# Up projections with the weights stationary and the rounded rows and remainders of both token tiles streamed as one; a norm's sums and the middle dilated group moved

## What is computed

```python
def first_block(x, ...):
    proj = rmsnorm(x, ln1_g) @ w_in            # qa ka va | qb kb vb | gates
    oa = dilated_attention(qa, ka, va)         # 12 heads of 64, three groups of 4, one per dilation
    ob = banded_attention(qb, kb, vb)          # 8 query heads, 2 key heads
    x = x + (sigmoid(ga) * (oa @ w_branch_a) + sigmoid(gb) * (ob @ w_branch_b)) @ w_out
    return x + square(relu(rmsnorm(x, ln2_g) @ w_up)) @ w_down      # 1024 -> 4096 -> 1024

def swiglu(x, w_in, w_out):                    # 1024 -> 2 x 2816 -> 1024
    gate, up = split(x @ w_in)
    return (silu(gate) * up) @ w_out

def second_block(x, ...):                      # two layers
    x = layer_norm(ALPHA * x + 0.5 * swiglu(x, ffn1), g0, b0)
    x = layer_norm(ALPHA * x + hybrid_mixer(x), g1, b1)
    x = layer_norm(ALPHA * x + 0.5 * swiglu(x, ffn2), g2, b2)
```

## Time and profile before

| | |
|---|---|
| median of 3 runs | 1364.85 us (1364.48 to 1365.22) |
| profiled execution | 1365.28 us, its span 1363.5 us |
| PE (matmuls) | 1343.1 us busy, 99%, 6449 instructions |
| PEld (weight loads) | 1090.2 us busy, 80% |
| DVE | 834.2 us busy, 61%, 1170 instructions |
| ACT | 633.7 us busy, 46%, 900 instructions |
| POOL | 67.4 us busy, 5% |
| DMA | 238.03 MB at 175 GB/s, the queue q1 at 53.5% |

### The profile page before, as it was taken

The page is one execution under the profiler, slowest core; times in us unless marked ns, Lnnn a source line. Parts: engine busy times, 40 slices in busy tenths (PEclk is TensorE's granted clock), DMA queues, the critical chain, the costliest instruction groups (busy, mean ns, idle before and its releaser), DMA issues.

```text
span 1363.5 us, 15986 instructions
## 1 busy us (share of the span) xinstructions
PE 1343.1 (99%) x6449; PEld 1090.2 (80%) x6449; DVE 834.2 (61%) x1170; ACT 633.7 (46%) x900; POOL 67.4 (5%) x133
## 2 busy tenths in 40 slices
PE   8999999999999999999999999999999999999997
PEld 7878788888888888876788888888888867888886
DVE  6676667454455555687874444754446888754445
ACT  7765635444335333346543334443344466444441
POOL 3130000000000000000300000000000002000000
PEclk9999999999999999999999999999999999999999
DMA  9542255555556655552465655475555442755650
GB/s 299 192 143 93 94 202 199 182 189 184 188 180 209 191 189 192 184 148 82 148 225 188 192 190 188 142 243 187 193 190 169 157 122 85 254 187 187 190 177 31
DMA packets 149241, 238.03 MB, mean 175 GB/s; under 512 B 5496, under 2 KB 97680, under 8 KB 149168
## 3 DMA queue, kind: packets, MB, share of 16 engines
q1 hardware_dynamic: 148784, 236.48, 53.5%
q0 software_dynamic: 384, 0.54, 0.2%
HBM read 235.95 MB, written 1.05 MB: 174 GB/s over the span
## 4 chain that ended last, share of the span: by engine, by line
PE 89%; DVE 5%; DVEq 1%; POOL 1%; ACT 1%; issue 1%; DMA 1%; POOLq 0%; SPq 0%; ACTq 0%
PE ps L1405 26%; PE ps L1407 25%; PE ps L1406 25%; PE ps L1742 2%; PE ps L1454 2%; PE ps L1447 1%; PE ps L1448 1%; PE ps L1653 1%; DVE stats L1166 1%; PE ps L1549 1%; PE ps L1575 1%; PE ps L1435 1%; POOL lrs L489 1%; DVE xres L1162 1%; PE ps L1666 1%
## 5 line engine op out<-in xcount | busy, mean ns | idle before, releaser
L462 DVE TENSOR_TENSOR wlo<-raw,whi 128x2048 fp32r<-128x2048 f32 x179 | 405.4, 2292 | 114.1 <-ACT whi L454 114.1
L1405 PE MATMUL ps<-whi,xt_hi 128*128 128x512 f32 (+1 forms) x1056 | 422.5, 400 | 0.5 <-DVE wlo L435 0.5
L1407 PE MATMUL ps<-whi,xt_lo 128*128 128x512 f32 (+1 forms) x1056 | 409.5, 388 | 0.0
L1406 PE MATMUL ps<-wlo,xt_hi 128*128 128x512 f32 (+1 forms) x1056 | 408.4, 387 | 0.0
L454 ACT ACTIVATE whi<-raw 128x2048 fp32r<-128x2048 f32 x197 | 370.4, 1915 | 0.0
L1405 PEld LDWEIGHTS ps<-whi,xt_hi 128*128 128x128 f32 x1056 | 198.6, 188 | 50.3 <-issue 13.9
L1407 PEld LDWEIGHTS ps<-whi,xt_lo 128*128 128x128 f32 x1056 | 198.4, 188 | 41.4
L1406 PEld LDWEIGHTS ps<-wlo,xt_hi 128*128 128x128 f32 x1056 | 199.0, 188 | 35.3
L776 ACT ACTIVATE ht_hi<-ps 128x256 fp32r<-128x256 f32 (+1 forms) x104 | 38.2, 415 | 323.8 <-PE ps L1742 323.6
L1405 PE MATMUL ps<-whi,ht_hi 128*128 128x512 f32 x480 | 187.7, 391 | 0.0
L1407 PE MATMUL ps<-whi,ht_lo 128*128 128x512 f32 x480 | 187.0, 390 | 0.0
(11 more groups left out here) (209 smaller groups left out, 1203.2 us busy)
## 6 DMA issues: line engine op xcount, KB each, us to landing
raw<-in_ffn_w_in_dram SPq DMA_DIRECT2D x176, 512.0 KB
raw<-in_ffn_w_out_dram SPq DMA_DIRECT2D x44, 1024.0 KB
raw<-in_w_in_dram SPq DMA_DIRECT2D x36, 1024.0 KB
raw<-in_w_up_dram SPq DMA_DIRECT2D x16, 1024.0 KB
raw<-in_w_down_dram SPq DMA_DIRECT2D x16, 1024.0 KB
raw<-in_w_out_dram SPq DMA_DIRECT2D x8, 1024.0 KB
raw<-in_w_out_dram SPq DMA_DIRECT2D x8, 512.0 KB
ln_g<-in_ln_g_dram SPq DMA_DIRECT2D x7, 512.0 KB, 8.0
```

The source lines that it names most:

```text
L462: dve.tensor_tensor(wlo[j][:, :], raw[j][:, :], whi[j][:, :].bitcast(F32), ALU.subtract).then_inc(lo_done, 1)
L1405: pe.matmul(o, hi[:, k, tok], block_of(whi, u, b, width), start=start, stop=False)
L1406: pe.matmul(o, hi[:, k, tok], block_of(wlo, u, b, width), start=False, stop=False)
L1407: return pe.matmul(o, lo[:, k, tok], block_of(whi, u, b, width), start=False, stop=stop)
```

## The change

**Up projections.** All chunks but the first of the MLP and of each feed-forward now have the weights as the stationary operand. A unit of weights holds 8 blocks x 256 columns instead of 4 x 512 (`load_columns`). `up_unit` takes 128 hidden columns of it: for each of 8 blocks one matmul with the rounded weights stationary and `xt_both` moving, which is the 256 tokens' rounded rows and their remainders, 512 columns in two runs of 256; and one with the weights' remainder stationary and the 256 rounded rows moving, into the first half of the same bank. The bank then holds 128 hidden columns x 256 tokens twice, and DVE adds the halves (`up_sum`). The hidden values are already transposed, so `hid_tile_pe` runs for the first chunks alone. In a feed-forward DVE adds gate columns and up columns, ACT takes silu from SBUF (`gate_act`), DVE multiplies; in the MLP DVE does relu and square in one instruction. ACT copies the rounded part, DVE the remainder (`ht_rest`). Banks are freed by a new semaphore, `up_read`.

**Norms.** The add sums its row as it goes (accum_out), DVE makes the mean, ACT squares and sums (`norm_act`), POOL does two operations (`rsqrt`), and the centred rows have a buffer of their own, `cent`. Ahead of three of the six norms, those behind a feed-forward that splits the next part's first two units early (`after`), DVE's order changes as well.

**Dilated groups.** The two heads of each pair of the middle group change places (`read_proj1`, strips 0 and 2), so its product comes from the other 64 rows, and the groups' scores are stored in the order 0, 2, 1, 256 columns apart. The scores of step HALF are issued behind that step's first filling pieces. DVE splits the units of the attention's steps in halves, at twice as many steps.

Cut to its core, the diff:

```diff
-STEP_LO = {2: 16, 4: 17, 6: 18, 8: 19, 10: 20, 13: 21, 15: 22, 17: 23}
+STEP_LO = {1: (16, 0), 2: (16, 1), 3: (17, 0), 4: (17, 1), 6: (18, 0), 7: (18, 1), 8: (19, 0), 9: (19, 1), 10: (20, 0),
+           11: (20, 1), 12: (21, 0), 13: (21, 1), 14: (22, 0), 15: (22, 1), 16: (23, 0), 17: (23, 1)}
+DIL_ORDER = (0, 2, 1)
...
-        xt_hi = sb("xt_hi", [P, KD, TOK], F32R, at=at_xt)
-        xt_lo = sb("xt_lo", [P, KD, TOK], F32R, at=at_xt + 8 * KB)
+        xt_both = sb("xt_both", [P, 2, KD, TOK], F32R, at=at_xt)
+        xt_hi, xt_lo = xt_both[:, 0], xt_both[:, 1]
...
+        def load_columns(sp, u, w, col):
+            load(sp, u, rows_of(u, KD), w[:, :, col:col + BW // 2])
         def load_ffn_in(sp, u, w, s):
+            if s > 0:
+                for c in range(2):
+                    load_columns(sp, u + c, w, c * FF2 + s * FFN_H)
...
-                load_strip(sp, mlp_up(s), w_up_r, s * BW)
+                if s == 0:
+                    load_strip(sp, mlp_up(s), w_up_r, s * BW)
+                else:
+                    for j in range(2):
+                        load_columns(sp, mlp_up(s) + j, w_up_r, s * BW + j * BW // 2)
...
+            if u < U_BRANCH:
+                m = scaled_lo(dve, u, (2 * h, 2 * h + 1))
+            else:
+                m = dve.tensor_tensor(wlo[j][:, part], raw[j][:, part], whi[j][:, part].bitcast(F32), ALU.subtract)
...
-                pool.tensor_tensor(lrs[:, t:t + 1], lrs[:, t:t + 1], half[:, 0:1], ALU.pow).then_inc(lrs_ready, 1)
+                rsqrt(pool, lrs[:, t:t + 1], mv[:, t, 1:2], 1.0 / DM, EPS2 / ALPHA ** 2, lrs_ready)
...
+        def norm_act(act, q, t):
+            act.wait_ge(mean_ready, 2 * q + t + 1)
+            act.activation(squares[:, t, :], xres[:, t, :], ACT.Square, bias=nmean[:, t:t + 1],
+                           accum_out=mv[:, t, 1:2]).then_inc(var_ready, 1)
...
+            elif s == 0:
+                parts = [plain(0, BW // 2)] + [swapped(BW // 2, i) for i in range(4)]
+            elif s == 2:
+                parts = [swapped(0, i) for i in range(4)] + [plain(BW // 2, BW)]
...
+        def gate_act(act, g):
+            act.wait_ge(up_read, 2 * up_index(g) + 1)
+            act.activation(hid_b[:, 0, :], hid_a[:, 0, :], ACT.Silu).then_inc(hid_act, 2)
...
+        def up_sum(dve, j, k, n):
+            b = UP_BANKS[j] + k
+            return dve.tensor_reduce(hid_a[:, j, k * TOK:(k + n) * TOK].rearrange("p (k n) -> p k n", k=n),
+                                     ps[:, b:b + n, :].rearrange("p k (j n) -> p k n j", j=2), AX.X, ALU.add)
+        def ht_rest(dve, g, par, k, n, src, done, by):
+            dve.wait_ge(ht_hi_done, 2 * g + done)
+            dve.tensor_tensor(ht_lo[par][:, k:k + n, :], src, ht_hi[par][:, k:k + n, :].bitcast(F32),
+                              ALU.subtract).then_inc(ht_lo_done, by)
...
+            dve.wait_ge(used, u + ffn_up(e) + 1)
+            up_sum(dve, 0, 0, 2).then_inc(up_read, 1)
             split_lo(dve, u + ffn_down(e))
+            for k in range(2):
+                cols = slice(k * TOK, (k + 1) * TOK)
+                if k == 0:
+                    dve.wait_ge(up_tile, g // FFN_S + 1)
+                else:
+                    dve.wait_ge(used, u + ffn_up(e) + 2)
+                m = up_sum(dve, 1, k, 1)
+                if k == 1:
+                    m.then_inc(up_read, 1)
+                dve.drain()
+                dve.wait_ge(hid_act, hid_acts(g + e) + 2)
+                dve.tensor_tensor(hid_b[:, 1, cols], hid_a[:, 1, cols], hid_b[:, 0, cols], ALU.mult).then_inc(hid_ready, 1)
+                if k == 1:
+                    for v in after[:1]:
+                        split_lo_half(dve, v, 0)
+                ht_rest(dve, g + e, e % 2, k, 1, hidden2[:, k:k + 1, :], k + 1, 1)
             for v in after[:1]:
-                split_lo(dve, v)
-            hidden_dve(dve, g + e, e % 2, True, (0,))
+                split_lo_half(dve, v, 1)
             for v in after[1:]:
                 split_lo(dve, v)
-            ht_dve(dve, g + e, e % 2, True, (0,))
...
-                dve.scalar_tensor_tensor(xs, src, (0.5 if ffn else 1.0) / ALPHA, xs, ALU.mult, ALU.add)
-            def stat(t, h):
+                dve.scalar_tensor_tensor(xs, src, (0.5 if ffn else 1.0) / ALPHA, xs, ALU.mult, ALU.add,
+                                         accum_out=sums[:, t, h:h + 1])
+            def mean(t):
                 dve.drain()
-                dve.bn_stats(stats[:, t, h, :], xres[:, t, h * BW:(h + 1) * BW])
-            def variance(t):
+                dve.tensor_scalar(nmean[:, t:t + 1], sums[:, t, 0:1], sums[:, t, 1:2], -1.0 / DM,
+                                  ALU.add, ALU.mult).then_inc(mean_ready, 1)
...
+                dve.scalar_tensor_tensor(cent[:, t, :], xres[:, t, :], nmean[:, t:t + 1], ln_g[:, :], ALU.add, ALU.mult)
...
-                parts = [(h % 2, 2 * g + h // 2, 6 + 2 * g + h // 2) for g in range(DIL_G)]
+                parts = [(h % 2 ^ (g == 1), 2 * g + h // 2, 6 + 2 * g + h // 2) for g in range(DIL_G)]
...
-                c = i * (n if len(parts) == DIL_G else BW)
+                c = DIL_ORDER.index(i) * TOK if u < HALF else i * BW
...
-        def up_chunk(pe, u, par, between=None, at=None):
-            for k in range(KD):
-                if k % 4 == 0:
-                    pe.wait_ge(lo_done, u + k // 4 + 1)
-                for t in range(TT):
-                    m = tile_mm(pe, xt_hi, xt_lo, k, u + k // 4, k % 4, t, 2 * par + t, k == 0, k == KD - 1)
-                if k % 4 == 3:
-                    m.then_inc(used, 1)
-                if k == at:
-                    between()
+        def up_unit(pe, u, j, k):
+            o = ps[:, UP_BANKS[j] + k, :]
+            pe.wait_ge(lo_done, u + 1)
+            for b in range(KD):
+                cols = slice(b * BW // 2 + k * P, b * BW // 2 + (k + 1) * P)
+                pe.matmul(o.rearrange("p (j n) -> p j n", j=2), whi[SLOT_OF[u]][:, cols], xt_both[:, :, b, :],
+                          start=b == 0, stop=False)
+                m = pe.matmul(o[:, 0:TOK], wlo[SLOT_OF[u]][:, cols], xt_hi[:, b, :], start=False, stop=b == KD - 1)
+            return m
+        def up_chunk(pe, u, g, first=None, tile=False):
+            for j in range(2):
+                for k in range(2):
+                    if first is not None and j == 1:
+                        hid_tile_pe(pe, g - 1, k, first)
+                    elif k == 0 and up_index(g) > 0:
+                        pe.wait_ge(up_read, 2 * up_index(g) - 1 + j)
+                    m = up_unit(pe, u + j, j, k)
+                    if k == 1:
+                        m.then_inc(used, 1)
+                    elif tile and j == 1:
+                        m.then_inc(up_tile, 1)
...
-                if i < UNITS:
+                if i < UNITS and i != HALF:
...
+                if i == HALF:
+                    scores(pe, i)
```

## The result

The changed kernel takes **1357.62 us** (median of 4 runs, 1356.41 to 1358.07) against 1365.03 beside it: a ratio of 0.9942, with a 95% interval of 0.9927 to 0.9958. It is faster by 7.4 us where 16.7 were forecast, and 1357.62 lies just above the range. This span is short for its time: 3.1 us of the execution lie outside it, 1.8 in the one before and 2.0 to 2.1 in the other three of the changed kernel. So 8.8 is some 1.3 more than the 7.5 by which the times of the same two executions differ.

What follows compares the result with a forecast made beforehand. PE's own queue was taken to bound the kernel, with room on DVE and ACT. The terms 9.9 - 24.2 - 3.0 - 0.4 + 1.4 - 0.4 = -16.7 us gave 1348.3 us, range 1344 to 1357.

Steps and rivals of the forecast that it cites:

- The up projections' matmuls: In 47 changed chunks, 32 x 226.7 + 32 x 119.8 = 11.09 us replaces 10.88: +9.9 us.
- The transposes: Hidden-tile transposes leave PE's queue except after first chunks, 0.89 us each in the MLP, 0.45 in feed-forwards: -24.2 us.
- The cover on DVE and ACT: The new sums and splits on DVE and ACT fit within each chunk's PE time in the steady part: zero.
- rival B: DVE's sums of PSUM values 256 elements apart take twice the price, costing 6.6 us: 1355 us; 12%.
- Scores: Dilated scores: with the middle group in the array's other half, three matmuls take 1.0 us, not 1.49: -3.0 us.
- D: Dilated scores gain nothing, as fp32 products in different array halves may not overlap across their two passes: 1351.3 us; 8%.
- The moved scores and halved splits: Scores of step HALF follow the filling pieces instead of waiting for the last transposed keys: -0.4 us (0 to -0.5).
- Swapped heads: ACT's first projection read becomes five instructions a tile instead of one; in strip 0 on the path: +1.4 us.
- The norms: Shorter norm chain (3.2 us instead of 3.6), but more DVE work before three norms: -0.4 us (-3 to +3).
- The wait in front: Behind three feed-forwards, PE waits 1.1 us for the first half of the normed rows.
- Rival A: Each wide up-projection matmul pays up to 13.0 ns for its operand's two segments: 19.6 us back, 1367.9 us, slower; 8%.
- Rival C: Weight loads don't hide behind narrow matmuls; slots as long as a load lose 105 us: 1453 us; 2%.

Runs made afterwards that it cites:

- The grouped order: Changed kernel with the 16 wide matmuls of a half chunk first, then the 16 narrow ones, instead of alternating: 1347.59 us, ratio 0.987.

## Why the prediction was wrong, point by point

**The step that failed is "The up projections' matmuls": 32 x 226.7 + 32 x 119.8 = 11.09.** Each pace was read from a stretch of one width and the two were added for a stream that alternates them. Measured is 11.29, so the term is 47 x (11.29 - 10.88) = +19.3 us instead of +9.9. The grouped order, with the same instructions, gives 11.10 and 1347.6, within 0.7 us of the 1348.3 forecast. The step was 9.4 us short and forecast and result are 9.3 apart; that the two agree so well, and that the grouped kernel lands so near the forecast, is in part luck, as the smaller misses below go both ways and nearly cancel. A hint may have been in the rows: behind the transposes, a narrow kind too, the next matmuls were late, which I put down to the transposes.

**The transposes.** They are gone as counted, 24.2 us, but the down projection starts on the slower pace: 0.06 a chunk, some 2.8 us back, no part of the sum.

**The cover on DVE and ACT** held. A sum over 1024 elements took 1.221 us where 1.22 was worked out, and one over 512 took 688 ns, with the added values 256 elements apart, where 687 stand in the earlier trace rows for neighbours. So strided PSUM reads cost nothing extra here, and rival B is out. The rule of the Trainium skill (Advanced Engine Details and Errata, "PSUM Cachelines"), which asks for contiguous pairs for best throughput, didn't show in this read. By form, the changed kernel's groups:

```profile
L1197 DVE TENSOR_REDUCE hid_a<-ps 128x512 f32<-128x1024 f32 x90 | 109.9, 1221 | 126.4 <-PE ps L1850 126.4
L1197 DVE TENSOR_REDUCE hid_a<-ps 128x256 f32<-128x512 f32 x8 | 5.5, 688 | 0.9 <-PE ps L1850 0.9
L813 ACT ACTIVATE squares<-xres,nmean 128x1024 f32<-128x1024 f32 x12 | 13.8, 1154 | 27.7 <-DVE nmean L1264 27.7
```

**Scores:** -2.6 where -3.0 stood; D is out. **The moved scores and halved splits:** -1.2 where -0.4 stood. Against the kernel with the heads unswapped, which starts its first scores within 0.1 us of before, the last ones come at 154.23 instead of 155.45; beside the 0.47 at step HALF, a wait of 0.49 for a maximum on DVE at the last unit went, which had no term. The table of half splits, which shortens what DVE does there in one piece, is the likely cause; no run changes it alone.

**Swapped heads:** +0.9 where +1.4 stood. ACT's ten small reads of strip 0 took 2.49 us in all instead of 1.27, and PE's wait went to 1.12. They answer to the earlier trace rows:

```profile
25.36 2.49 ACT L638 ACTIVATE proj<-ps,lrs 128x256 f32<-128x256 f32 x10 [3.77 <-POOL lrs L528]
30.32 5.40 DVE L476 SCALAR_TENSOR_TENSOR wlo<-raw,g_cols,whi 128x512 fp32r<-128x512 f32 x8 [1.77 <-ACT whi L469]
33.21 0.47 PE L1499 MATMUL ps<-whi,xt_both 128*128 128x512 f32 x1 [1.12 <-DVE wlo L476]
```

**The norms:** -2.4 where -0.4 stood, inside its range of -3 to +3. The chain from the second add to the scale is 3.25 us (3.2 counted), in the changed kernel's timeline:

```profile
564.90 0.68 DVE L1259 SCALAR_TENSOR_TENSOR xres<-ps,xres 128x512 f32<-128x512 f32 x1
...
565.91 1.16 ACT L813 ACTIVATE squares<-xres,nmean 128x1024 f32<-128x1024 f32 x1 [4.09 <-DVE nmean L1264]
...
567.58 0.54 POOL L528 TENSOR_TENSOR lrs<-lrs,half 128x1 f32<-128x1 f32 x1
568.15 1.42 DVE L1276 SCALAR_TENSOR_TENSOR xres<-cent,lrs,ln_b 128x512 f32<-128x512 f32 x2 [0.89 <-POOL lrs L528]
```

The wait in front was to be 1.1 and is 0.39 three times: the splits ended at 17.5 as walked, but DVE was through its two adds 0.4 us sooner (1.3 us for both instead of 1.6), and PE with its matmuls 0.4 us later. The second wait is 0.26 to 0.28 as said (0.3), five times; for the two behind the attention the prediction had none. At the end the scale starts 3.36 us behind PE's last matmul (4.5 in the earlier trace rows, 3.4 forecast):

```profile
1347.03 0.39 PE L1501 MATMUL ps<-whi,ht_lo 128*128 128x512 f32 x1
...
1350.78 1.42 DVE L1276 SCALAR_TENSOR_TENSOR xres<-cent,lrs,ln_b 128x512 f32<-128x512 f32 x2 [0.89 <-POOL lrs L528]
```

**The sum by measured terms:** 19.3 - 24.2 + 2.8 - 2.6 - 1.2 + 0.9 - 2.4 = -7.4 us, against -8.8 by the spans. The 1.4 that remain are small differences spread over the kernel. From the last transposes ahead of it to the next norm's first, each of the first three feed-forwards takes 179.2 us before and 179.5 now, with the wait of 0.39 in it, so nothing is lost where the terms have 10 x (0.41 - 0.45 + 0.06) = +0.2; the MLP takes 3.3 us less where they have 7 x (0.41 - 0.89 + 0.06) = -2.9; and from the last scale to the end of the span it is 3.9 us instead of 4.2. Rival A came nearest in size and for the wrong reason: a price of some 6 ns on each wide matmul, half of its bound, but for what stands before it and not for what it reads. Rival C's price for a slot as long as a load is excluded, as no slot grew to a load's length. The rule of the Trainium skill behind it (TensorE: Matmul & The Clock Gate, Part 3, "What overlaps and what doesn't": loads overlap only in other row groups) doesn't fit these rows, where 97 loads of full height fit into 11.52 us of narrow matmuls without a gap. The sum that the prediction made by that rule was too large besides: a chunk has 64 loads where it had 48, so 16 x 47 = 752 are added and not 1504, 80 us at 107 ns each and not 161.

**What stays open** is what in the engine makes a lone shorter matmul between longer ones cost 6 ns (at 256 and 384 columns) or 11 (at 448), and why two in a row lose half as much a change. A second segment and the bank are excluded by runs, and an uncovered load as far as the estimated paces at 384 and 448 columns hold. The columns that stream in and the columns written to the bank change together in every run here, so which of them counts is not shown.

## What to carry to other kernels

A pace read from a uniform stretch holds for a uniform stretch. Where a change mixes shapes, price the mixture as an unknown of its own, bounded by the nearest place in the trace where one kind follows the other, and try the order in groups before giving up a form: here the same instructions, sorted by width, are worth 10 us of 1357.6. And work put ahead of a chain that PE waits for can cost more than the result shows, when another part of the same change shortens that chain: undo the parts one at a time.

## What was not expected of the hardware

- A pair of one wide matmul (512 columns) and one narrow (256) takes 352.8 ns where they alternate one by one, 348 in twos, 347 in sixteens, with 346.5 as the sum of the pure paces; all at a granted clock of 1.00.
- Narrow matmuls slow the next handful of matmuls of 512 columns from 0.227 to as much as 0.24 us apiece, 0.06 us in all behind an alternating stretch and 0.03 behind sixteen narrow ones.
- A moving operand in two runs of 256 columns, 8 KB apart, streams like one run of 512: chunks take 11.29 us with either, and 32 such matmuls alone start 0.2266 us apart.
- A VectorE sum of pairs that lie 256 elements apart in PSUM takes 688 ns over 512 elements, where a reduction over neighbours took 687.
- Score products of 64 rows in three instructions take 1.49 us from one half of the array and 1.06 with the middle one from the other half.
